# Twenty-eight more products on TensorE behind the last one of a decoder layer, in seven layouts of their operands

## Time and profile before

| | us |
|---|---|
| median of 3 runs | 1394.96 |
| lowest and highest run | 1394.67, 1395.44 |
| the profiled execution's own time | 1395.06 |
| its span, first to last instruction | 1393.4 |
| TensorE busy | 1388.3 (100%) |
| VectorE busy | 857.0 (62%) |
| ScalarE busy | 583.3 (42%) |
| GpSimd busy | 130.7 (9%) |
| HBM traffic | 236.60 MB, mean 170 GB/s |

### The profile page before, as it was taken

The page is one execution under the profiler, slowest core; times in us unless marked ns, Lnnn a source line. Parts: engine busy times, 40 slices in busy tenths (PEclk is TensorE's granted clock), DMA queues, the critical chain, the costliest instruction groups (busy, mean ns, idle before and its releaser), DMA issues.

```text
span 1393.4 us, 28677 instructions
## 1 busy us (share of the span) xinstructions
PE 1388.3 (100%) x10755; PEld 1375.1 (99%) x10755; DVE 857.0 (62%) x1178; ACT 583.3 (42%) x707; POOL 130.7 (9%) x214
## 2 busy tenths in 40 slices
PE   9999999999999999999999999999999999999999
PEld 9999999999999999999999999999999999999999
DVE  7778877657876555555554445555555556667554
ACT  7556744665334333333333333333333333335332
POOL 1523105001221000000000000000000001111000
PEclk9999999999999999999999999999999999999999
DMA  8756435446554545545445556545454545556553
GB/s 298 204 186 233 142 130 174 143 141 227 181 170 162 166 165 165 166 156 173 159 144 163 163 162 196 168 157 170 156 170 161 165 131 163 164 161 197 184 158 117
DMA packets 76905, 236.60 MB, mean 170 GB/s; under 512 B 14136, under 2 KB 14672, under 8 KB 76472
## 3 DMA queue, kind: packets, MB, share of 16 engines
q1 hardware_dynamic: 72072, 223.43, 50.2%
q0 software_dynamic: 3744, 11.22, 2.7%
q10 hardware_dynamic: 1040, 1.28, 0.3%
HBM read 231.34 MB, written 4.47 MB: 169 GB/s over the span
## 4 chain that ended last, share of the span: by engine, by line
PE 98%; ACT 1%; DVE 1%; DMA 0%; issue 0%; SPq 0%; DVEq 0%; ACTq 0%
PE acc L516 31%; PE acc L518 30%; PE acc L517 30%; PE px L1551 0%; PE px L1669 0%; PE px L1511 0%; PE px L1514 0%; PE px L1517 0%; DMA w_raw<-in_w_in 0%; PE px L1609 0%; PE px L516 0%; PE px L518 0%; PE px L517 0%; PE px L1736 0%; ACT w_hi L462 0%
## 5 line engine op out<-in xcount | busy, mean ns | idle before, releaser
L468 DVE TENSOR_TENSOR w_lo<-w_raw,w_hi 128x1024 fp32r<-128x1024 f32 (+3 forms) x446 | 509.8, 1148 | 313.9 <-ACT w_hi L462 305.0
L462 ACT ACTIVATE w_hi<-w_raw 128x1024 fp32r<-128x1024 f32 (+3 forms) x446 | 439.5, 988 | 551.2 <-PE acc L518 544.3
L516 PE MATMUL acc<-n_hi,w_hi 128*128 128x288 f32 x1664 | 492.5, 296 | 0.0
L517 PE MATMUL acc<-n_lo,w_hi 128*128 128x288 f32 x1664 | 490.9, 295 | 0.0
L518 PE MATMUL acc<-n_hi,w_lo 128*128 128x288 f32 x1664 | 489.2, 294 | 0.0
L518 PEld LDWEIGHTS acc<-n_hi,w_lo 128*128 128x128 f32 x1664 | 313.5, 188 | 0.0
L517 PEld LDWEIGHTS acc<-n_lo,w_hi 128*128 128x128 f32 x1664 | 312.4, 188 | 0.0
L516 PEld LDWEIGHTS acc<-n_hi,w_hi 128*128 128x128 f32 x1664 | 311.8, 187 | 0.0
L516 PE MATMUL acc<-x_hi,w_hi 128*128 128x288 f32 x816 | 244.9, 300 | 0.0
L517 PE MATMUL acc<-x_lo,w_hi 128*128 128x288 f32 x816 | 240.8, 295 | 0.0
L518 PE MATMUL acc<-x_hi,w_lo 128*128 128x288 f32 x816 | 240.0, 294 | 0.0
(11 more groups left out here) (304 smaller groups left out, 889.9 us busy)
## 6 DMA issues: line engine op xcount, KB each, us to landing
w_raw<-in_w_gu SPq DMA_DIRECT2D x176, 512.0 KB, 3.9
w_raw<-in_w_in SPq DMA_DIRECT2D x76, 512.0 KB, 4.3
w_raw<-in_w_down SPq DMA_DIRECT2D x64, 384.0 KB, 3.1
w_raw<-in_w_down SPq DMA_DIRECT2D x64, 320.0 KB, 3.1
w_raw<-in_w_ple SPq DMA_DIRECT2D x32, 576.0 KB, 3.7
w_raw<-in_w_out SPq DMA_DIRECT2D x32, 512.0 KB, 4.2
w_raw<-in_w_in SPq DMA_DIRECT2D x12, 256.0 KB, 6.2
proj<-in_xT SPq DMA_DIRECT2D x8, 288.0 KB, 6.6
```

The source lines that it names most:

```text
L462: nc.scalar.activation(whi[:, slot, 0:kt * P], raw[:, slot, 0:kt * P], ACT.Copy).then_inc(S("w_hi_done"), 1)
L468: nc.vector.tensor_tensor(wlo[:, slot, 0:kt * P], raw[:, slot, 0:kt * P], whi[:, slot, 0:kt * P].bitcast(F32), ALU.subtract).then_inc(S("w ...
L516: nc.tensor.matmul(out, w_h, row_of(m_hi_, k0 + k), start=first and k == 0, stop=False)
L517: nc.tensor.matmul(out, w_h, row_of(m_lo_, k0 + k), start=False, stop=False)
```

## The change

Behind the last `ple` tile, TensorE's program gets 28 more products. They read `n_hi` on both sides and write bank 3 of `px`, which nothing reads any more. They wait for no semaphore and raise none. There are seven kinds, four products of each, in this order:

1. 288 neighbouring columns moving, 128 weight columns (the form of the products before);
2. every second column moving, 288 of them;
3. 288 neighbouring columns that begin one element later;
4. two pieces of 144 columns, 288 apart;
5. one column, read 288 times;
6. as 1, with 32 weight columns, so 32 output partitions;
7. 512 neighbouring columns, with 32 weight columns.

```diff
             for j in range(2):
                 ple(N_OUT // 2 - 1, j, at_end=j == 1)
 
+            flat_n = n_hi[:, 0:4, :].rearrange("p a t -> p (a t)")
+            pairs_n = flat_n.rearrange("p (t z) -> p t z", z=2)
+            halves_n = flat_n[:, 0:2 * T].rearrange("p (z t) -> p z t", z=2)
+            for moving, stationary, parts in ((flat_n[:, 0:T], n_hi[:, 4, 0:P], P), (pairs_n[:, 0:T, 0], n_hi[:, 4, 0:P], P),
+                                              (flat_n[:, 1:T + 1], n_hi[:, 4, 0:P], P), (halves_n[:, :, 0:T // 2], n_hi[:, 4, 0:P], P),
+                                              (flat_n[:, 0:1].broadcast_to([P, T]), n_hi[:, 4, 0:P], P),
+                                              (flat_n[:, 0:T], n_hi[:, 4, 0:32], 32), (flat_n[:, 0:512], n_hi[:, 4, 0:32], 32)):
+                for _ in range(4):
+                    M(px[0:parts, 3, 0:512 if moving.shape[-1] == 512 else T], stationary, moving, start=True, stop=True)
+
```

## The result

The changed kernel takes 1396.54 us as the median of 20 runs (1395.96 to 1397.33), the kernel before 1394.70 (1394.25 to 1395.65) in the same comparison. The ratio is 1.0013, with a 95% interval of 1.0007 to 1.0019: 1.8 us slower, inside the 0.2% that I counted as no change. 1396.4 was forecast, 1.4 us above before. The profiled execution took 1396.79 us, its span 1395.1 against 1393.4 before.

The account below looks back on a forecast made before the run. TensorE bounds the body, but SyncE's store ends last. The 28 products take 4.4 us, about 2.7 covered, so the span grows 1.4 to 1394.8; plus 1.7 for the execution, less 0.1 for the median: 1396.4 us, range 1395.3 to 1397.9.

Parts of the forecast that it names:

- The order of arrival: At the block's end, SyncE's drain stays at 1393.2 and TensorE's, over at 1390.5 before, now closes later, at 1394.63.
- the cover: Behind TensorE's last product, VectorE's tail, the store and its landing hide about the first 2.7 us of added products.
- The sum: TensorE's new products, first start 1390.24 to last end 1394.56; 2.7 us or so covered, so the span grows 1.4 us.
- rival A in its small form: In the new products, one or two kinds go at half rate: 1396.8 to 1397.7; chance 0.16, shared with the clock's fall.
- the change of width: Between 128 and 32 weight columns in the new products: 0.05 us once, the middle, since the recorded rows change type too.
- The rule on lines: For every second column moving: each 16-byte line is hit twice, so no extra cost, against 0.43 us at half rate.
- The 131 ns: For the 512-column products: a second rule would make the sum 0.3 us shorter; set aside for the trace's 0.23 us.
- B (the clock): Clock falls under the narrow products, kinds 6 and 7 at half rate: 1.3 us more, 1397.7; chance 0.16, shared with half-rate kinds.
- C (nothing shows): At the end, SyncE and stores alone decide, or products go faster: 1395.0; chance 0.09, shared with dropped or joined products.
- D (dropped or joined): The new products are dropped as unread or joined as alike: 1395.0; chance 0.09, shared with nothing showing.

## Why the prediction was right

**The order of arrival** at the end was the heart of it, and held: SyncE kept its place against the rest (0.16 us earlier, like all of this execution), TensorE came last, and 16 products fit under the cover for nothing while 28 on the path cost 4.9 us.

**The sum** came out at 4.32 us from the first new start to the last end (1390.24 to 1394.56; the 4.4 us in its words are a slip); it was 4.78 (1390.08 to 1394.86). The term that was mis-sized is kind 2: I took 0.133 us for each of kinds 2 to 5, "rows 5 are the nearest, in type, columns and weights; what differs is only the address pattern". The address pattern is what costs: 0.253, so 0.48 us for the four, the half rate that I had priced at 0.43 and put into rival A in its small form. The other deviations are under 0.05 us each and nearly cancel: the first product behind those of 144 columns is 0.18 from the next, kind 5 takes 0.123, and the change of width, 0.05 in my sum, costs nothing in the split form here.

**The rule on lines.** The Trainium skill, page "SBUF — State Buffer", section "Door 1: The DMA port swizzle", asks for two hits to a 16-byte line. I cited it for kind 2 at no cost. The runs contradict it for TensorE's moving side in two types of three: two hits to a line cost two cycles a column in every type (0.253 us split form, 0.250 at 16 bits, 0.254 plain), and only in plain float32, whose normal rate that is (0.248), are they enough. The split form and 16 bits were back at the full rate with four to a line; three weren't tried. The measurement decides. The 131 ns that the Trainium skill gives for 512 columns (page "TensorE: Matmul & The Clock Gate", section "Back-to-back issue gap") were rightly set aside: kind 7 took 0.23 us.

**Around the sum:** the drain at most 0.05 us behind the last product (0.07 taken), 0.2 to the end of the span (0.2), the execution 1.7 us above the span (1.7). The new span was 1395.1, not 1394.8. The 0.46 us that the sum was short show in the span as 0.3, since this execution reached the new products 0.16 us early. The median grew by 1.8 us against 1.4, a difference of the size of kind 2's 0.48. That the absolute figure is only 0.14 off is luck, as the kernel before is 0.26 us faster in the longer series. So is that the median lies in the band that the prediction gave to all forms at the rate of rows 5 and 9 (1395.9 to 1396.8): one form was not at that rate.

**The rivals.** A in its small form is what happened, in one kind of seven. B (the clock) did not: granted clock 1.00. Nor did C (nothing shows): the time grew, and TensorE's drain closes last. Nor D (dropped or joined): TensorE has 10783 records, 28 more than before.

## What to carry to other kernels

Read first who arrives last at the end: work behind an engine's last useful instruction is free up to the gap to that arrival, and costs its length beyond it. For TensorE's operands, count how many columns of the stream fall into each 16-byte line: in the split form a moving side of every second column doubles a product, and a weight side of every fourth one makes the load the bound. And where TensorE bounds a kernel with split-form products, weave two halves of the moving columns and take them apart in the eviction, which was free on VectorE: 6.8% here.

## What the runs showed of the hardware

One set of numbers fits all moving sides that were run to within some 6%, though the readers themselves are inferred. A line read anew costs a reader 4.2 cycles at 2.4 GHz (1.76 ns). The worst fits are neighbouring columns, 0.133 us, and 0.136 when they begin one later (the first distance left out), where the estimate from this price is 0.127 and 0.128. Plain float32 and 16-bit moving columns behave as with one reader, as weights do; the split form as with two, on alternate columns. A reader goes back and forth between two lines at about 2 cycles a step plus 2.1 for each line newly read (20.2 cycles for 8 columns give 0.304 us, 36.2 for 16 give 0.272; measured 0.304 and 0.274). Neighbouring split-form columns ask for a new line every four cycles, just at the limit. That this costs the 0.005 to 0.011 us by which they lag behind woven, repeated and doubled columns (0.1225 to 0.128) is argued from the model; that weaving takes it away is shown, in the tail and over 2447 products of the body.
